# Six of eleven pairs of the down projection as seven block products, lower halves split between two engines

## The reference

```python
for l in range(DEPTH_2):
    ...
    h2 = rmsnorm(x, norm2_g[l])
    f_gate, f_up = jnp.split(h2 @ w_ffn_in[l], 2, axis=-1)
    x = x + (jax.nn.silu(f_gate) * f_up) @ w_ffn_out[l]
return x
```

## Time and profile before

| | us |
|---|---|
| median of 3 runs | 1244.17 (1244.05 to 1244.55) |
| profiled execution, span | 1242.9 |
| PE busy | 1239.0 |
| DVE busy | 957.8 |
| ACT busy | 722.1 |
| POOL busy | 422.0 |
| down stage n = 1 (784.27 to 841.40), n = 2 (1182.70 to 1239.83) | 57.13 each |

### The profile page before, as it was taken

The page is one execution under the profiler, slowest core; times in us unless marked ns, Lnnn a source line. Parts: engine busy times, 40 slices in busy tenths (PEclk is TensorE's granted clock), DMA queues, the critical chain, the costliest instruction groups (busy, mean ns, idle before and its releaser), DMA issues.

```text
span 1242.9 us, 17085 instructions
## 1 busy us (share of the span) xinstructions
PE 1239.0 (100%) x6634; PEld 1061.2 (85%) x6634; DVE 957.8 (77%) x1377; ACT 722.1 (58%) x1023; POOL 422.0 (34%) x338
## 2 busy tenths in 40 slices
PE   9999999999999999999999999999999999999999
PEld 8988788888888889888888888888988888888887
DVE  6875667677887478986878888986898597888895
ACT  7755545376765365577836555546457674655552
POOL 0010012039892069377420112008746750012100
PEclk9999999999999999999999999999999999999999
DMA  9753334555555448644554554465855454555442
GB/s 360 274 195 136 136 119 169 173 199 187 197 179 201 170 170 267 214 155 176 175 210 175 183 190 162 176 220 185 289 180 193 154 174 165 203 183 190 162 166 114
DMA packets 39008, 233.75 MB, mean 188 GB/s; under 512 B 4752, under 2 KB 5392, under 8 KB 13072
## 3 DMA queue, kind: packets, MB, share of 16 engines
q1 hardware_dynamic: 38928, 232.67, 53.4%
HBM read 225.31 MB, written 1.05 MB: 182 GB/s over the span
## 4 chain that ended last, share of the span: by engine, by line
PE 100%; DVE 0%; issue 0%; POOL 0%; POOLq 0%
PE ps L657 19%; PE ps L564 18%; PE ps L566 18%; PE ps L565 18%; PE ps L662 10%; PE ps L569 6%; PE ps L583 2%; PE ps L625 1%; PE ps L624 1%; PE ps L623 1%; PE ps L725 1%; PE ps L1209 1%; PE ps L700 0%; PE ps L893 0%; PE ps L810 0%; PE ps L811 0%
## 5 line engine op out<-in xcount | busy, mean ns | idle before, releaser
L1299 ACT ACTIVATE whi<-raw 128x2048 fp32r<-128x2048 f32 (+1 forms) x212 | 400.2, 1891 | 115.0 <-PE ps L566 101.5
L2052 DVE TENSOR_TENSOR wlo<-raw,whi 128x2048 fp32r<-128x2048 f32 x168 | 388.0, 2315 | 90.0 <-ACT whi L1299 89.3
L1885 POOL TENSOR_TENSOR wlo<-raw,whi 128x512 fp32r<-128x512 f32 x176 | 229.1, 1337 | 88.6 <-ACT whi L1299 85.6
L657 PE MATMUL ps<-hh,whi 128*128 128x512 f32 x1056 | 255.8, 391 | 0.0
L657 PEld LDWEIGHTS ps<-hh,whi 128*128 128x128 f32 x1056 | 193.0, 188 | 36.5
L564 PE MATMUL ps<-whi,hh 128*128 128x512 f32 (+1 forms) x504 | 201.3, 399 | 0.0
L566 PE MATMUL ps<-whi,hh 128*128 128x512 f32 (+1 forms) x504 | 195.5, 388 | 0.0
L565 PE MATMUL ps<-wlo,hh 128*128 128x512 f32 (+1 forms) x504 | 195.1, 387 | 0.0
L1857 POOL TENSOR_TENSOR st<-st,sm 128x1 f32<-128x1 f32 (+2 forms) x28 | 45.2, 1614 | 391.5 <-DVE st L2106 228.0
L662 PEld LDWEIGHTS ps<-hh,wlo 128*128 128x128 f32 x1056 | 137.8, 191 | 6.7
L662 PE MATMUL ps<-hh,wlo 128*128 128x256 f32 x1056 | 139.8, 282 | 0.0
(11 more groups left out here) (348 smaller groups left out, 2061.6 us busy)
## 6 DMA issues: line engine op xcount, KB each, us to landing
raw<-in_w SPq DMA_DIRECT2D x202, 1024.0 KB, 4.9
raw<-in_w SPq DMA_DIRECT2D x12, 256.0 KB, 6.7
gain<-in_bias SPq DMA_DIRECT2D x12, 256.0 KB, 5.0
kst<-kh SPq DMA_DIRECT2D x16, 128.0 KB, 2.8
qst<-qh SPq DMA_DIRECT2D x16, 128.0 KB, 2.3
raw<-in_w SPq DMA_DIRECT2D x2, 560.0 KB, 10.8
x<-in_x SPq DMA_DIRECT2D x4, 256.0 KB, 5.7
gain<-in_rows SPq DMA_DIRECT2D x2, 512.0 KB, 5.6
```

The costliest lines, as they stand in the source:

```text
L657: pe.op.matmul(o[:, :], wh[:, k, c], t.hh[:, k, :, :], start=k == 0, stop=False, skip_group_check=True)
L1299: act.op.activation(t.whi[i % NHI][:, c], t.raw[i % NRAW][:, c], ACT.Copy).then_inc(*at("act_hi", ("hi", i)))
L1885: pool.op.tensor_tensor(t.wlo[i % NRAW][:, half(k)], t.raw[i % NRAW][:, half(k)], t.whi[i % NHI][:, half(k)].bitcast(F32), ALU.subtract).t ...
L2052: dve.op.tensor_tensor(t.wlo[i % NRAW][:, c], t.raw[i % NRAW][:, c], t.whi[i % NHI][:, c].bitcast(F32), ALU.subtract).then_inc(*at("dve_lo ...
```

## The change

Pairs 2 and 6 join `SEVEN`. A list `POOL_DN` gives POOL, in n = 1 and n = 2, the lower halves of the chunks of pairs 1, 2, 3, 5, 6, 7 (of these the 1536 columns of the raw part, three instructions) and of 8, 9, 10 (four instructions). DVE keeps pairs 0 and 4 and the summed parts of all six. The weight sums of a pair no longer stand at its own raw chunk: DVE makes them as soon as it comes to the place ahead of it, so that between neighbouring seven-product pairs they stand before the lower half of the earlier pair's sums. POOL waits for the sums before it overwrites a raw part. The data sums get two more tiles each.

```diff
-SEVEN = (1, 3, 5, 7)
+SEVEN = (1, 2, 3, 5, 6, 7)
...
+POOL_DN = (1, 2, 3, 5, 6, 7, 8, 9, 10)
+POOL_LO |= {UNITS[f"dn{n}"][c] for n in (1, 2) for c in POOL_DN}
...
-    t.gsh, t.gsl = ([at(f"{w}{c}", p + o + (4, 8, 40, 30)[c], [128, 4, 128], R32) for c in range(len(SEVEN))]
+    t.gsh, t.gsl = ([at(f"{w}{c}", p + o + (4, 8, 0, 21, 40, 30, 34)[c], [128, 4, 128], R32) for c in range(len(SEVEN))]
...
         pool.wait_ge(*on("hi", i))
-        for k in range(4):
+        if i + 1 in SUMS:
+            pool.wait_ge(*on("raw", i + 1))
+        for k in range(1 if i + 1 in SUMS else 0, 4):
...
             g_sums(l + 1, c)
+        for c in POOL_DN:
+            split(UNITS[f"dn{l + 1}"][c])
...
+        if i in summed:
+            return
+        summed.add(i)
         src, dst = t.raw[i % NRAW], t.raw[(i + 1) % NRAW]
+        dve.wait_ge(*on("raw", i))
         dve.wait_ge(*on("used", i + 1 - NRAW))
...
             i = upto[0]
             upto[0] += 1
+            for m in (i, i + 1) if i in SUMS else (i,):
+                if m + 1 in SUMS:
+                    weight_sums(m)
+                    await_own()
             if i in POOL_LO:
                 continue
             dve.wait_ge(*on("raw", i))
-            if i + 1 in SUMS:
-                weight_sums(i)
-                await_own()
             dve.wait_ge(*on("hi", i))
```

More of the change, by code:

```diff
@@ L2023, in first_splits @@
         upto[0] = i + 1
+    summed = set()
     def weight_sums(i):
+        if i in summed:
+            return
+        summed.add(i)
         src, dst = t.raw[i % NRAW], t.raw[(i + 1) % NRAW]
+        dve.wait_ge(*on("raw", i))
         dve.wait_ge(*on("used", i + 1 - NRAW))
```

## The result

The changed kernel takes 1285.95 us (median of 4 runs, 1284.76 to 1286.57), the kernel before 1244.36 us (4 runs, 1244.05 to 1244.81): a ratio of 1.0333, interval 1.032 to 1.0346. It is 41.6 us slower; +41.5 us and 1285.7 us were predicted. The profiled execution took 1284.76 us around a span of 1283.5 us, so 1.3 us lie outside the span, as before.

A forecast was written before the change was run, and what follows sets the result against it. PE's matmuls were taken to bound the kernel; turns at a port shared by DVE and POOL add +21.4 us in layer 0 and +20.1 in layer 1, saved products included: 1244.17 + 41.5 = 1285.7 us, 8-in-10 range 1270 to 1299.

The forecast's parts named there:

- What bounds the kernel: Whole kernel: PE busy 1239.0 of 1242.9 us, so only fewer matmuls or PE waits count; saved products give -2.72 us.
- Up stages at 0: Up stages: two more sets of data sums per layer on ACT and POOL cost 0, at most 4.4 us.
- The exclusion and its prices: Down stages: DVE and POOL SBUF instructions take turns; a piece costs DVE 1.1 us, a lower half costs POOL 2.2.
- Pairs 2 and 3: Layer 0's down stage: PE waits 3.2 us at pair 2's sums and 5.2 us at pair 3's raw part.
- Pair 6: Layer 0's down stage: PE waits 1.4 us for POOL's pieces and 0.8 us for the lower half of the sums.
- Pair 7 and chunks 8 to 10: Layer 0's down stage: waits of 3.1 us at pair 7, then 0.3, 3.8 and 4.9 us at chunks 8, 9, 10.
- Layer 1's end: Layer 1, chunks 8 to 10: waits 0.3 + 1.1 + 6.3 us in place of 0.3 + 3.8 + 4.9; layer +20.1 us.
- Rival 3, the clock: Down stages: PE granted 1.2 in place of 2.4 GHz behind stalls, +13.6 us, some hidden, about 1295 us; chance 0.10.
- some 22 us a layer: Expected profile of after: PE's waits in each layer's down stage, released by POOL's and DVE's lower halves, some 22 us.
- Rival 1: Down stages: the port matters little, only POOL's pace at the end counts, +5.2 us, 1249.4 us; chance 0.07.
- Rival 2: Down stages: all lower halves in time, -2.72 us, 1241.5 us; chance 0.03.
- Rival 4: Down stages: the products are not saved; given nothing, since the instruction lists have 12 matmuls less.

The follow-up runs named there:

- Experiment 8: The changed kernel with SEVEN = (1, 3, 5, 6, 7) and POOL_DN empty, so everything in the down stages on DVE: 1244.30 us, ratio 1.0002.
- experiment 5: The changed kernel with POOL_DN = (1, 2, 3, 5, 6, 7) and each raw part one POOL instruction of 1536 columns: 1267.99 us, ratio 1.0191.
- experiment 6: The changed kernel with POOL_DN = (1, 2, 3, 5, 6, 7), DVE's lower halves of sums and chunk 4 in four 512-column instructions: 1273.22 us, ratio 1.0233.
- experiment 2: The changed kernel with only the raw parts on POOL, chunks 8 to 10 back on DVE: 1275.77 us, ratio 1.0253.
- experiment 4: The changed kernel with SEVEN = (1, 3, 5, 7) as before and only those pairs' raw parts on POOL: 1245.38 us, ratio 1.0008.
- experiment 7: The changed kernel with small matmuls of zeros on PE ahead of its long waits: 1281.08 us, ratio 1.0297.
- experiment 3: The changed kernel with SEVEN = (1, 3, 5, 7) as before and only chunks 8 to 10 on POOL: 1254.93 us, ratio 1.0091.
- experiment 1: The changed kernel with POOL_DN empty, all lower halves of the down stages on DVE: 1247.50 us, ratio 1.0026.

## Why the prediction was right, point by point

- **What bounds the kernel.** Right: 12 matmuls less, and everything else is PE's waits and clock. Experiment 8 shows how tight it is: 0.9 us of lateness on a transpose outweighs three matmuls.
- **Up stages at 0.** Right: the stage starts 0.1 us from where it did, and no wait is in the up stages. It was closer than the prediction has it: in experiments 5 and 6 PE waits 2.8 and 1.8 us at pair 1 for DVE's last up-stage steps, which POOL's work for pair 2 holds up.
- **The exclusion and its prices.** Right: DVE's lower half 3.38 us, POOL's pieces 3.2 to 3.3. The Trainium skill, page SBUF — State Buffer, section "SBUF: two separate sides", calls it an exclusive lock for the whole instruction; the trace agrees in kind. In size the trace has 1.10 us a piece, as the row that the prediction went by (1.11), and not 1.26: with a piece between them DVE's lower halves start 3.30 us apart (799.24 and 802.54) in place of 2.20. That the time came out near 1286 and not near 1291 does not show this, since the total has misses that cancel (below). Experiments 2, 5 and 6 show turns by the instruction, and 4 shows them where they cost nearly nothing. That it is a port that is shared is the page's statement; the runs show only who waits for whom.
- **Pairs 2 and 3.** Close. DVE's small steps end at 794.4 (794.75 predicted), the lower half of pair 2's sums at 799.32 (799.65), pair 3's raw part at 807.04 (807.60). The idle time at pair 3 is 3.1 us in place of 5.2, since PE came to it late: its matmuls ran at half the clock from 799.4 on.
- **Pair 6.** Missed: 1.4 + 0.8 us predicted, no wait seen, since PE came later than reckoned. With the clock mostly full, in experiment 7, the two places lose 0.5 + 0.7 us: the terms were also 1 us too large; why stays open.
- **Pair 7 and chunks 8 to 10.** PE goes on at 832.32 and at 851.04; the predicted terms, added up along the stage, give 832.7 and 851.9. Chunk 8 has no wait (0.3), chunk 9 one of 1.45 us (3.8), chunk 10 one of 4.87 (4.9).
- **Layer 1's end.** Mis-sized: one wait of 3.22 us where 1.1 + 6.3 was reckoned, with slow matmuls in part of its place. The layer gave some +18.5 us, +20.1 was predicted.
- **Rival 3, the clock.** Its mechanism was there, its sum was not. By the prediction's own list a granted clock under 1.0 behind the stalls would show it wrong in this point, and it was 0.50 to 0.54 behind eight of the nine. The prediction kept it out of its own sum, and gave it +13.6 us on top of the waits, of which some is hidden: about 1295. The slow time is of that size (8.1 + 7.5 us), but it does not stand on top: where PE next waits for a lower half whose time DVE and POOL set, a slow matmul is taken out of that wait. So the sentence "some 22 us a layer" of waits fell: layer 0 has 14.3 us in its idle rows and layer 1 11.4, with 8.1 and 7.5 in slow starts.
- **The size of the waits.** Here lies a miss that the total hides. Experiment 7 shows the waits with the clock mostly full, counted from one real matmul to the next. Layer 0: 2.7, 4.9, 0.5, 0.7, 2.8, 3.0 and 5.0 us at pairs 2, 3, 6 (two places), 7 and chunks 9 and 10, where the steps gave 3.2, 5.2, 1.4, 0.8, 3.1, 3.8 and 4.9; that is 19.6 us against 22.8 with chunk 8 (the eight terms as printed sum to 22.7). Layer 1: 16.2 us against some 21.4, and 3 us of that difference is its end. The chain by hand was too long by 3 us in layer 0 and 5 in layer 1. The slow matmuls that it left out add about as much: 3.6 us that experiment 7 still has and the 4.9 us that it gave back. That the sum met the median within 0.3 us is luck, these two misses cancelling; the mechanism, turns that make PE wait through both down stages, was right.
- **Rivals 1, 2 and 4** fell: experiment 2 stands 34 us from what POOL's pace would give; PE waits nine times; the products are saved.

Open: whether lower halves that DVE reads from PSUM would free POOL, as the gate stage suggests. It was not tried, and no PSUM space was looked for.

## What to carry to other kernels

Before work is moved from VectorE to GpSimd, find a stretch of the trace where both have SBUF operands at once, and add their two times on one resource: here 8.3 us a pair against 4.76 us of TensorE. With a plain pair between (experiment 4) the same sum is 8.3 + 2.2 us against 10.2, and the move cost 1 us; with the pairs next to one another (experiment 2) it cost 28. And when the bound engine has no slack, the ceiling is the work it saves, here 2.7 us of 1244, while any engine that is made later by a microsecond takes it back.

## What the runs showed of the hardware that was not expected

- Behind eight of the nine waits of the changed kernel, those of 2.3 to 4.9 us, PE was granted 0.50 to 0.54 of its clock, for 3 to 6 us. The length of a wait did not settle it alone: behind one of 2.45 us (experiment 3, layer 1) and one of 2.31 us (experiment 6, 1235.57) the clock stayed at 1.00, as behind those of 1.45 us (843.16) and 1.53 us (experiment 1). Nor did the fall come at once each time: behind the wait at pair 7 PE ran 1.6 us at the full clock first. The Trainium skill, page TensorE: Matmul & The Clock Gate, Part 1, has idleness bring the lower level back; the trace agrees in kind.
- Matmuls of zeros in the waits, such as 28 of 128 columns in 1.74 us, kept the clock at 1.00 in both down stages, but for 3.3 us at 0.50 behind the last wait of layer 0 (2.16 us of idle time after 48 of them). They were worth 4.9 us, since most of the slow time lay ahead of other waits.
- Turns are by instruction, not by bytes: three pieces of 512 columns beside long DVE instructions took 9.8 us, one of 1536 took 5.4, and three beside DVE instructions of 512 took 4.9.
